# A hybrid attention and expert layer on one core: GpSimd makes each expert tile's low part in two instructions of 512 columns instead of one of 1024

## The chip, the cores and the metric

The kernel runs on one core of a Trainium2 chip. The metric is the device time of one execution in microseconds (us), as the median of several runs. The core has a matrix engine (PE, with its weight loads shown as PEld), a vector engine (DVE), a scalar engine (ACT), GpSimd (POOL) and a queue engine that issues DMAs (SP). They run side by side and wait for one another by semaphores.

## The reference

One layer over 512 tokens of width 1024 in float32: two kinds of attention, an output projection and a layer norm, then an expert layer ("peer") over 16384 experts, each one row of `u` and one of `v`. Cut to the part that matters here:

```python
qb = (xb @ w_q).reshape(TOKEN_BLOCK, PEER_HEADS, 2, PEER_DKEY)
s = jnp.einsum('thcd,hcnd->thcn', qb, sub_keys).astype(jnp.float32)
s_top, i_top = lax.top_k(s, PEER_TOPK)
cand = s_top[:, :, 0, :, None] + s_top[:, :, 1, None, :]
...
best, pos = lax.top_k(cand, PEER_TOPK)
eidx = jnp.take_along_axis(cand_idx, pos, axis=-1)
g = jax.nn.softmax(best, axis=-1)
h = jax.nn.gelu(jnp.einsum('td,thkd->thk', xb, ug).astype(jnp.float32), approximate=False)
return jnp.einsum('thk,thkd->td', (g * h).astype(x.dtype), vg)
```

Per token 16 experts are chosen for each of 8 heads, and their `u` and `v` rows are used. The expert layer's result goes through a last layer norm.

## The kernel before

**Products in three parts.** Each float32 operand of a product is split into a high part (`whi`, `xhi`, made by ACT as a rounded copy) and a low part (`wlo`, `xlo`, the raw value less the high part). The product is the sum of three matmuls: high by high, and twice high by low (`split`, L1306 to L1308).

**The expert stage.** For 384 of the 512 tokens the kernel doesn't gather: it multiplies with all 128 tiles of `u` (128 experts each) and later with all 128 tiles of `v`. A list `SEQ` gives the order of these 256 steps. For each step `s`, SP loads a tile of 128x1024 into `raw` (L513, four slots), ACT makes its high part (`tile_high`, L804), then `tile_low` makes the low part: GpSimd for the first 38 tiles (`POOL_ONLY = 38`, L627), DVE from tile 38 on (L1172). PE waits for the low part (`wait_low`) and runs 24 matmuls of 384 columns (`u_tile`); ACT takes the result through GELU into `hout` (`gelu`, L825) and then makes the high part of the tile four steps ahead. A `u` step of PE lasts 4.16 us.

**Which experts each token wants.** While PE runs the first of these steps, DVE picks the experts: the largest 16 of 128 scores for each head and half (L1078 to L1087), and then `select`, four times (once for each 128 tokens), in six parts. It builds candidate sums (`cand`, L1122), takes the largest 16 (L1126 to L1138), and turns positions into expert numbers by comparisons, products and sums over 128x1920 elements of bf16: `ge` (L1142, L1150), `prod` (L1143, L1147, L1152), `sel` (L1144, L1148, L1153), with short steps between them (L1114, L1140, L1145, L1149, L1154, L1156). DVE's instructions here form one chain in program order.

**What DVE does next.** Behind `select` DVE's program goes on in steps, from step 37: for the first 128 tokens it forms dot products with gathered `u` rows (`dots`, L1180), for which ACT computes the GELU (L840, `dots_gelu`), and adds up `v` rows (`sums`, L1194). It makes the low parts of tiles 38, 39 and so on, and from step 46 one-hot matrices of the chosen experts (`one_hots`, ending in `e1w`, L1211), from which PE forms gate weights (`g_quad`, L1597). ACT's program has `dots_gelu` for step 37 ahead of `gelu(35)`, and PE can't start `u_tile(37)` before `gelu(35)` has emptied its bank of PSUM.

**GpSimd's program in this stage**: `tile_low(0)` to `tile_low(37)`; behind each of `tile_low(26)` to `tile_low(30)` one gather of `u` and `v` rows (L634, an indirect DMA); then 123 further gathers, each waiting for DVE's sums.

Of the kernel before, what the change touches and what calls it, by code (L numbers as in the profile page):

```python
# [23 lines left out]
F32 = mybir.dt.float32  # L24
# [4 lines left out]
ALU = mybir.AluOpType  # L29
# [4 lines left out]
S, D = 512, 1024  # L34
# [127 lines left out]
def program(nc, a):  # L162

    es = ExitStack()
    with es:
# [168 lines left out]
        raw4, whi4, wlo4 = [t[:, :, :].rearrange("p a (b c) -> p (a b) c", b=2) for t in (raw, whi, wlo)]  # L334

        def slot4(n):

            return (n + 2) % 4
# [4 lines left out]
        def sem(name):  # L343
            return es.enter_context(nc.semaphore(name))
# [32 lines left out]
        tile_hi, low_pool, low_dve = sem("tile_hi"), sem("low_pool"), sem("low_dve")  # L377
# [205 lines left out]
        @block.gpsimd  # L583
        def _(pool):
            nc.gpsimd.memset(ident[:, :], 0.0).then_inc(id_steps, 1)
            pool.wait_ge(id_steps, 1)
            nc.gpsimd.affine_select(out=ident[:, :], in_=ident[:, :], compare_op=ALU.not_equal, fill=1.0,
                                    base=0, pattern=[[-1, P]], channel_multiplier=1).then_inc(id_steps, 1)

            def low(g, cols=GC):  # L590

                pool.wait_ge(hi_done, g + 1)
                s = g % 2
                nc.gpsimd.tensor_tensor(wlo[:, s, 0:cols], raw[:, s, 0:cols],  # L594
                                        whi[:, s, 0:cols].bitcast(F32), ALU.subtract).then_inc(lo_done, 1)

            for i in range(4):
                cols = slice(i * GC // 4, (i + 1) * GC // 4)
                if i < 3:
                    pool.wait_ge(first_hi, i + 1)  # L600
                else:
                    pool.wait_ge(hi_done, 1)
                nc.gpsimd.tensor_tensor(wlo[:, 0, cols], raw[:, 0, cols], whi[:, 0, cols].bitcast(F32),
                                        ALU.subtract).then_inc(first_lo if i < 3 else lo_done, 1)
            for g in range(2, G_BR):
                low(g)

            low(G_BR, 6 * 256)
            low(G_BR + 1, 6 * 256)
            for m in range(KD):  # L610
                if m in (2, 4):
                    low(G_BR + m // 2 + 1, 6 * 256)
                pool.wait_ge(mix_hi, m + 1)
                nc.gpsimd.tensor_tensor(xlo[:, m, :], mixa[:, m % 2, :], xhi[:, m, :].bitcast(F32), ALU.subtract).then_inc(mix_lo, 1)
            low(G_WO + 1)
            low(G_WO + 2)
            pool.wait_ge(ln_out, TC)
            for g in range(G_WQ, G_U):
                low(g)

            nc.gpsimd.iota(iota2[:, :, :], [[1, P], [0, 2]], base=0, channel_multiplier=0,
                           allow_small_or_imprecise_dtypes=True).then_inc(iota_done, 1)

            def tile_low(n):

                pool.wait_ge(tile_hi, n + 1)
                nc.gpsimd.tensor_tensor(wlo4[:, slot4(n), :], raw4[:, slot4(n), :], whi4[:, slot4(n), :].bitcast(F32),  # L627
                                        ALU.subtract).then_inc(low_pool, 1)

            def gather(k):  # L630

                if k >= UVB:
                    pool.wait_ge(sum_done, k - UVB + 1)
                nc.gpsimd.indirect_dma_start(  # L634
                    out=uvb[:, k % UVB, :], out_offset=None, in_=a["uv"][:, :],
                    in_offset=bass.IndirectOffsetOnAxis(ap=eidx[:, k:k + 1], axis=0)).then_inc(uv_in[k % UVB], 16)

            for s in range(POOL_ONLY):
                tile_low(s)
                if s == GATHER_TILE:  # L640
                    pool.wait_ge(idx_done, 1)
                if GATHER_TILE <= s < GATHER_TILE + UVB:
                    gather(s - GATHER_TILE)
            for k in range(UVB, NG):
                gather(k)
# [1064 lines left out]
```

## Time and profile before

| what | value |
|---|---|
| median of 3 runs | 1626.87 us (1626.55 to 1627.24) |
| the profiled execution's own time | 1627.04 us |
| its span in the trace | 1624.9 us |
| PE busy | 1607.9 us, 99% of the span |
| DVE busy | 1239.0 us, 76% |
| ACT busy | 637.8 us, 39% |
| POOL busy | 463.7 us, 29% |
| granted PE clock | full speed in every slice of the page |
| L627, the low parts by GpSimd | 38 instructions, 95.0 us, from 494.2 to 652.4 us |

Busy time is the time in which an engine executes instructions. An instruction that stands waiting for a memory port inside the engine is still shown as busy, so that its duration grows; a wait for a semaphore is shown as idle time in front of it.

### The profile page before, as it was taken

To read this page: it belongs to the slowest core of one execution; us is meant where nothing else is said; L and a number is where in the kernel's file an instruction comes from. 1 tells how busy PE (TensorE), PEld (TensorE's weight loads), DVE (VectorE), ACT (ScalarE), POOL (GpSimd) and SP (SyncE) were. 2 spreads that over 40 slices of the span, in tenths; PEclk is the share of its full clock that TensorE was granted. 3 is DMA by queue.
4 is the path that set the end of the run, shared out by engine and by line. 5 is a ranking of instruction groups with operands and counts; after the bars stand their busy time and mean duration, and the time that the engine had idled before them with its cause. 6 is when DMAs were issued, how large, how long until landed. Compare 5 with 4: busy or idle time off the path is not lost.

```text
span 1624.9 us, 24287 instructions
## 1 busy us (share of the span) xinstructions
PE 1607.9 (99%) x9533; PEld 1430.0 (88%) x9533; DVE 1239.0 (76%) x2317; ACT 637.8 (39%) x998; POOL 463.7 (29%) x218
## 2 busy tenths in 40 slices
PE   9999999999999999999999999999999999999997
PEld 8898977888889999999999999999998888888886
DVE  3024366246799999998887799989998898888887
ACT  5324445532223343445455343333333434333332
POOL 4433222351244567300000233333333121222200
PEclk9999999999999999999999999999999999999999
DMA  5332112143124558788788999999999999999961
GB/s 201 146 149 79 55 53 78 59 150 130 53 78 137 177 169 303 275 278 275 245 272 250 402 373 387 396 392 358 357 387 388 366 381 384 373 365 384 392 245 66
DMA packets 135137, 406.56 MB, mean 250 GB/s; under 512 B 10353, under 2 KB 71025, under 8 KB 113777
## 3 DMA queue, kind: packets, MB, share of 16 engines
q1 hardware_dynamic: 116592, 270.80, 46.0%
q0 software_dynamic: 18432, 134.23, 21.0%
q8 instruction: 76, 1.25, 0.3%
q14 instruction: 37, 0.30, 0.1%
HBM read 360.42 MB, written 44.56 MB: 249 GB/s over the span
## 4 chain that ended last, share of the span: by engine, by line
PE 80%; DVE 18%; issue 1%; DMA 1%; POOL 0%; ACT 0%; DVEq 0%; SPq 0%; POOLq 0%
PE bank L1306 24%; PE bank L1308 24%; PE bank L1307 24%; PE bank L1597 3%; DVE idx L1087 1%; DVE idx L1079 1%; DVE val L1078 1%; DVE val L1086 1%; DVE tmp L1080 1%; DVE prod L1143 1%; PE bank L1448 1%; PE bank L1435 1%; DVE prod L1152 1%; PE bank L1405 1%; DVE wlo L1172 1%
## 5 line engine op out<-in xcount | busy, mean ns | idle before, releaser
L1306 PE MATMUL bank<-xhi,whi 128*128 128x384 f32 (+1 forms) x1408 | 499.0, 354 | 1.9 <-ACT hout L825 1.8
L1308 PE MATMUL bank<-xhi,wlo 128*128 128x384 f32 (+1 forms) x1408 | 492.6, 350 | 0.0
L1307 PE MATMUL bank<-xlo,whi 128*128 128x384 f32 (+1 forms) x1408 | 492.0, 349 | 0.0
L634 POOL DMA_INDIRECT uvb<-in_uv,eidx x128 | 201.4, 1573 | 696.8 <-DVE acc L1194 666.3
L804 ACT ACTIVATE whi<-raw 128x1024 fp32r<-128x1024 f32 x256 | 270.2, 1057 | 250.8 <-PE bank L1308 223.5
L1172 DVE TENSOR_TENSOR wlo<-raw,whi 128x1024 fp32r<-128x1024 f32 x218 | 266.0, 1222 | 77.4 <-ACT whi L804 76.8
L1308 PE MATMUL bank<-whi,alo 128*128 128x512 f32 x768 | 299.5, 390 | 0.0
L1307 PE MATMUL bank<-wlo,ahi 128*128 128x512 f32 x768 | 299.4, 390 | 0.0
L1306 PE MATMUL bank<-whi,ahi 128*128 128x512 f32 x768 | 298.7, 389 | 0.0
L1306 PEld LDWEIGHTS bank<-xhi,whi 128*128 128x128 f32 x1408 | 264.5, 188 | 18.5 <-issue 3.5
L1307 PEld LDWEIGHTS bank<-xlo,whi 128*128 128x128 f32 x1408 | 264.6, 188 | 15.2
L1308 PEld LDWEIGHTS bank<-xhi,wlo 128*128 128x128 f32 x1408 | 264.3, 188 | 15.4
L594 POOL TENSOR_TENSOR wlo<-raw,whi 128x2048 fp32r<-128x2048 f32 (+1 forms) x33 | 149.2, 4522 | 298.5 <-ACT whi L654 263.2
L1308 PEld LDWEIGHTS bank<-whi,alo 128*128 128x128 f32 x768 | 144.2, 188 | 29.9
L1306 PEld LDWEIGHTS bank<-whi,ahi 128*128 128x128 f32 x768 | 144.2, 188 | 29.3
L1307 PEld LDWEIGHTS bank<-wlo,ahi 128*128 128x128 f32 x768 | 144.2, 188 | 29.3
L825 ACT ACTIVATE hout<-bank 128x384 f32<-128x384 f32 x128 | 62.8, 491 | 272.2 <-PE bank L1308 270.4
L1194 DVE SCALAR_TENSOR_TENSOR acc<-uvb,hd,acc 128x1024 f32<-128x1024 f32 x127 | 163.2, 1285 | 4.5
L1180 DVE CUSTOM_DVE_ANT_0 uvb<-uvb,xn 128x1024 f32<-128x1024 f32 x128 | 151.3, 1220 | 0.0
L627 POOL TENSOR_TENSOR wlo<-raw,whi 128x1024 fp32r<-128x1024 f32 x38 | 95.0, 2504 | 61.7 <-ACT whi L804 61.6
L847 ACT ACTIVATE ahi<-af 128x384 fp32r<-128x384 f32 x128 | 66.5, 520 | 83.4 <-DVE af L1225 83.4
L1231 DVE TENSOR_TENSOR alo<-af,ahi 128x384 fp32r<-128x384 f32 x128 | 70.7, 552 | 0.0
(197 smaller groups left out, 1742.9 us busy)
## 6 DMA issues: line engine op xcount, KB each, us to landing
raw<-in_u SPq DMA_DIRECT2D x128, 512.0 KB, 6.3
raw<-in_uv SPq DMA_DIRECT2D x128, 512.0 KB, 8.4
g_scratch<-stage SPq DMA_DIRECT2D x48, 512.0 KB, 5.3
gl<-g_scratch SPq DMA_DIRECT2D x32, 768.0 KB, 9.3
raw<-in_w_in SPq DMA_DIRECT2D x22, 1024.0 KB, 4.8
h_scratch<-hout SPq DMA_DIRECT2D x88, 192.0 KB, 4.9
hl<-h_scratch SPq DMA_DIRECT2D x22, 768.0 KB, 10.4
raw<-in_w_q SPq DMA_DIRECT2D x6, 1024.0 KB, 4.8
```

Source lines behind the costliest of these rows:

```text
L594: nc.gpsimd.tensor_tensor(wlo[:, s, 0:cols], raw[:, s, 0:cols], whi[:, s, 0:cols].bitcast(F32), ALU.subtract).then_inc(lo_done, 1)
L627: nc.gpsimd.tensor_tensor(wlo4[:, slot4(n), :], raw4[:, slot4(n), :], whi4[:, slot4(n), :].bitcast(F32), ALU.subtract).then_inc(low_pool, 1)
L634: nc.gpsimd.indirect_dma_start(out=uvb[:, k % UVB, :], out_offset=None, in_=a["uv"][:, :], in_offset=bass.IndirectOffsetOnAxis(ap=eidx[:, ...
L804: nc.scalar.activation(whi4[:, slot4(n), :], raw4[:, slot4(n), :], ACT.Copy).then_inc(tile_hi, 1)
L847: nc.scalar.activation(ahi[:, t % 4, :], af[:, t % 4, :], ACT.Copy).then_inc(a_hi, 1)
L1172: V.tensor_tensor(wlo4[:, slot4(n), :], raw4[:, slot4(n), :], whi4[:, slot4(n), :].bitcast(F32), ALU.subtract).then_inc(low_dve, 1)
L1180: V.tensor_tensor_reduce(out=u, in0=u, in1=xn[:, 0, :], scale=1.0, scalar=0.0, op0=ALU.mult, op1=ALU.add, accum_out=hd[:, k:k + 1]).then_i ...
L1194: V.scalar_tensor_tensor(acc[:, :], v, hd[:, k:k + 1], acc[:, :], ALU.mult, ALU.add).then_inc(sum_done, 1)
L1231: V.tensor_tensor(alo[:, p % 4, :], af[:, p % 4, :], ahi[:, p % 4, :].bitcast(F32), ALU.subtract).then_inc(a_lo, 1)
L1306: mm(out, lh, rh, start=first, stop=False)
L1307: mm(out, lh, rl, start=False, stop=False)
L1308: return mm(out, ll, rh, start=False, stop=last)
```

## The change

In GpSimd's `tile_low`, one subtraction over the tile's 1024 columns becomes two over 512 columns each, in a loop. The first one has no semaphore; the second one carries the increment of `low_pool` that the whole tile had. The wait for ACT's high part stays in front of the first. Nothing else is changed; DVE's own `tile_low` stays whole.

```diff
             def tile_low(n):
 
                 pool.wait_ge(tile_hi, n + 1)
-                nc.gpsimd.tensor_tensor(wlo4[:, slot4(n), :], raw4[:, slot4(n), :], whi4[:, slot4(n), :].bitcast(F32),
-                                        ALU.subtract).then_inc(low_pool, 1)
+                for j in range(2):
+                    o = (slice(None), slot4(n), slice(j * S, (j + 1) * S))
+                    last = nc.gpsimd.tensor_tensor(wlo4[o], raw4[o], whi4[o].bitcast(F32), ALU.subtract)
+                last.then_inc(low_pool, 1)
```

`S` is 512. On GpSimd, the place behind the last weights of the earlier stages and up to the second gather, as the two programs' instructions stand (all line numbers behind L627 are two higher after the change):

```order
 L621 IOTA iota_106 128x256
-L627 TENSOR_TENSOR wlo<-raw,whi 128x1024 x27
-L634 DMA uvb<-in_uv,eidx 128x2048
-L627 TENSOR_TENSOR wlo<-raw,whi 128x1024
...
+L629 TENSOR_TENSOR wlo<-raw,whi 128x512 x54
+L636 DMA uvb<-in_uv,eidx 128x2048
+L629 TENSOR_TENSOR wlo<-raw,whi 128x512 x2
+L636 DMA uvb<-in_uv,eidx 128x2048
```

27 instructions become 54 ahead of the first gather, and two stand between gathers where one stood. The instructions of the other engines and their order stay as they were.

## Rows read from the trace of the kernel before

**Rows 1.** Busy time by stretch: PE, PEld, DVE, ACT, POOL, each with instructions (x)

```profile
494.00:660.00 166.00, 166.00 (x954) 164.23 (x953) 160.15 (x529) 58.75 (x80) 101.57 (x43) 1.00 0.60 194
```

**Rows 2.** PE's waits, whole span: us in total, times, longest

```profile
PE bank L1597 <- DVE e1w L1211: 1.3, 1, 1.3
```

**Rows 3.** Timeline, PE around its first stop: start us, us

```profile
660.63 0.34 PE L1308 MATMUL bank<-xhi,wlo 128*128 128x384 f32 x1
662.80 0.41 PE L1306 MATMUL bank<-xhi,whi 128*128 128x384 f32 x1 [1.83 <-ACT hout L825]
```

**Rows 4.** Timeline, ACT at the same place

```profile
662.08 0.20 ACT L840 ACTIVATE hgel<-hd 128x2 f32<-128x2 f32 x1 [7.95 <-DVE hd L1180]
```

**Rows 5.** The instructions of L627: ns min/median/max; what ended POOL's idle time

```profile
L627 POOL TENSOR_TENSOR wlo<-raw,whi x38: 2382/2392/3531, 494.2 to 650.0; 128x1024 fp32r<-128x1024 f32 x38
...
  ACT whi L804: 61.6, 32
```

**Rows 6.** The instructions of L614, the same operation over 512 columns

```profile
L614 POOL TENSOR_TENSOR xlo<-mixa,xhi x8: 1290/1296/1301, 328.6 to 357.6; 128x512 fp32r<-128x512 f32 x8
```

**Rows 7.** Timeline, DVE, 533 to 659 us

```profile
533.60 3.00 DVE L1122 TENSOR_TENSOR cand<-val 128x64 f32<-128x64 f32 x6
...
544.39 2.16 DVE L1142 TENSOR_TENSOR ge<-bposf,cstb 128x1920 bf16<-128x1920 bf16 x1
546.58 3.31 DVE L1143 TENSOR_TENSOR prod<-ge,didx 128x1920 bf16<-128x1920 bf16 x1
...
566.32 3.19 DVE L1122 TENSOR_TENSOR cand<-val 128x128 f32<-128x128 f32 x7
...
599.40 0.99 DVE L1122 TENSOR_TENSOR cand<-val 128x128 f32<-128x128 f32 x7
...
607.06 0.23 DVE L1140 CAST bposf<-bpos 128x128 bf16<-128x128 uint32 x1
...
654.80 1.23 DVE L1152 TENSOR_TENSOR prod<-ge,didx 128x1920 bf16<-128x1920 bf16 x1
...
658.25 0.29 DVE L1154 TENSOR_TENSOR picks<-sel,idf 128x128 f32<-128x128 f32 x1
```

**Rows 8.** Timeline, POOL, 494 to 627 us

```profile
494.16 4.75 POOL L627 TENSOR_TENSOR wlo<-raw,whi 128x1024 fp32r<-128x1024 f32 x2 [5.78 <-ACT whi L804]
...
546.04 2.77 POOL L627 TENSOR_TENSOR wlo<-raw,whi 128x1024 fp32r<-128x1024 f32 x1 [1.77 <-ACT whi L804]
...
600.12 2.52 POOL L627 TENSOR_TENSOR wlo<-raw,whi 128x1024 fp32r<-128x1024 f32 x1 [1.77 <-ACT whi L804]
...
616.23 0.95 POOL L634 DMA_INDIRECT uvb<-in_uv,eidx  x1 [0.16 <-issue]
...
624.60 1.76 POOL L634 DMA_INDIRECT uvb<-in_uv,eidx  x1
```

**Rows 9.** Groups by form, DVE, 494 to 655 us: busy us, mean ns of one

```profile
L1143 DVE TENSOR_TENSOR prod<-ge,didx 128x1920 bf16<-128x1920 bf16 x4 | 13.2, 3306 | 0.1
L1152 DVE TENSOR_TENSOR prod<-ge,didx 128x1920 bf16<-128x1920 bf16 x4 | 11.1, 2787 | 0.1
...
L1114 DVE TENSOR_TENSOR didx<-idf 128x240 bf16<-128x240 bf16 x4 | 3.3, 817 | 0.1
L1140 DVE CAST bposf<-bpos 128x128 bf16<-128x128 uint32 x4 | 3.2, 805 | 0.1
L1145 DVE TENSOR_TENSOR picks<-sel,idf 128x128 f32<-128x128 f32 x4 | 3.1, 768 | 0.1
...
L1154 DVE TENSOR_TENSOR picks<-sel,idf 128x128 f32<-128x128 f32 x3 | 2.3, 773 | 0.1
L1149 DVE TENSOR_TENSOR jf<-bposf,sel 128x128 bf16<-128x128 bf16 x4 | 2.3, 578 | 0.1
```

**Rows 10.** Timeline, DVE and POOL near 20 us

```profile
18.33 4.36 DVE L898 CAST xplo<-xlo 128x512 fp32r<-128x512 f32 x8
...
21.18 6.00 POOL L594 TENSOR_TENSOR wlo<-raw,whi 128x2048 fp32r<-128x2048 f32 x1 [7.47 <-ACT whi L654]
```

## The prediction

> **What bounds the kernel now.** I read the busy times by stretch first. In the 166 us in which the changed instructions run, PE is busy for all 166.00 us and POOL for 101.57 [rows 1]. So PE doesn't wait for a low part there, and POOL, at 1.77 us idle behind most tiles, has room; what ends its idle time is ACT's high part, 32 times of 38 [rows 5]. A longer or shorter `tile_low` costs PE nothing by itself: a tile is made some three `u` steps (12.5 us) before PE wants it.
>
> But DVE is busy for 160.15 of the 166 us [rows 1], with one chain of instructions, and behind it stand two stops of PE. The first: ACT waited 7.95 us for DVE's dot products, which come straight after `select` [rows 4], so that its GELU came late, and PE started a matmul at 662.80 us whose predecessor had started at 660.63 [rows 3]. Matmuls of this form start 0.17 us apart, so 2.0 us are lost, and 0.1 on the slow first one. The second, 1.3 us, is for DVE's `e1w` [rows 2], some 37 us later in the same unbroken chain. So DVE's arrival at the end of `select` (659.6 us) is on the path. If DVE gets there X earlier, PE gains X, up to 2.1 + 1.3 = 3.4 us; behind that PE alone bounds. If DVE gets there later, PE loses the same, with no cap.
>
> **Why GpSimd's instruction length touches DVE at all.** `prod<-ge,didx` takes 1.23 us when GpSimd is through with its tiles, and 3.31 us at 546.58, as in seven of its eight executions [rows 7, 9]. At 546.04 a low part of GpSimd started; DVE's `ge` (L1142) ran until 546.55; the low part lasts 2.77 us instead of 2.39 and ends at 548.81; DVE's product ends at 549.89, 1.08 us behind it [rows 7, 8]. So each waits for the other's whole instruction: GpSimd 0.4 us for `ge`, then DVE 2.08 us for GpSimd. The two want one thing that only one can hold, and GpSimd had asked for it before the product did. In the Trainium skill, "SBUF — State Buffer", section "Who interferes with whom", this is an exclusive lock on a port pair, taken by a DVE instruction with two SBUF inputs against a GpSimd one that reads SBUF; the rows agree, and the sum by it is the sum below.
>
> What DVE loses so, by its rows in `select` less their own durations: L1143 13.2 - 4 x 1.23 = 8.3; L1152 11.1 - 4 x 1.23 = 6.2; L1114 3.3 - 4 x 0.30 = 2.1; L1140 3.2 - 4 x 0.23 = 2.3; L1145 3.1 - 4 x 0.29 = 1.9; L1154 2.3 - 3 x 0.29 = 1.4; L1149 2.3 - 4 x 0.29 = 1.1 [rows 7, 9]; L1122, whose seven take 0.99 us undisturbed and twice 2.2 us more, 4.4 [rows 7]. Together 27.8 us.
>
> **The change, part by part.**
>
> *GpSimd's own time.* The same operation over 512 columns took 1.29 us [rows 6], over 1024 2.39 [rows 5]: two make 2.58, 0.19 us more per tile, 7 us over 38 tiles. Idle time of 1.77 us per tile hides it; without that cover it would be 7 us. Even if both halves have to let a long DVE instruction through (2.58 + 2.2 + 1.2 = 6.0 us), the tile is done before PE's 12.5 us are over.
>
> *What DVE waits, where it waits.* If DVE, waiting, gets in between the halves, a product's wait falls from 2.08 to what the first half holds: 1.29 less the 0.12 us in which it starts up, less the 0.15 that DVE's own start hides and the 0.03 between DVE's instructions, about 0.98. Seven products: 7 x (2.08 - 0.98) = 7.7 us less.
>
> *What that gives back.* The second half still has to run, and stands waiting when DVE's product ends. It takes the port then, and whatever DVE does 1 to 3 us later meets it. I laid DVE's instructions of 533 to 660 us end to end on this rule, each with its own duration, and GpSimd's halves at ACT's ends, which PE's 4.16 us step fixes. With whole instructions this gives the 23 waits of the trace and its end, 659.6 us. With halves it gives 34 waits: the products fall by 7.7; L1145, L1149 and L1154, short ones behind a product, fall from 4.4 to 2.9; L1140 stays at 2.4. But L1147, which always ran free between two low parts, is met three times (2.9); L1142 and L1150 once each (2.0); L1156 twice (2.2); and the heads of `select` (L1122, L1114), a burst of short instructions that one whole low part stopped three times for 6.5 us, are stopped eight times for 8.7. Sum: -7.7 - 1.5 + 2.9 + 2.0 + 2.2 + 2.2 = +0.1 us, within rounding. DVE ends at 659.8.
>
> *Why the end is so stiff.* After each wait DVE continues when a GpSimd instruction ends, and these stand on PE's 4.16 us grid. So DVE's chain doesn't drift; it comes out at one of a few places. Moving the start-up times and the half's length by a few hundredths left it at +0.1 to +0.2 in most cases, at +0.5 in some, and in some at -3.0 to -3.2, where the last head of `select` slips through. I take +0.1.
>
> *Sum.* 1627.04 (the profiled execution; the median is 0.17 lower) + 0.0 for GpSimd + 0.1 for DVE = 1627.1; against the median, 1627.0 us. Bounds for DVE's term: -3.4 (the cap; all else that it saves finds PE bound) and +3.9 (rival 2).
>
> **The rivals.** *0, the forecast: DVE gets in between the halves, and gives back what it saves.* 1627.0 us. For it: the gather that GpSimd issued right behind a low part at 624.60 took 1.76 us, where the one at 616.23 took 0.95 [rows 8]; a product of DVE that had waited for that low part ran first, and the gather stood behind it. Between two halves GpSimd must start up as well, so a waiting DVE should win.
>
> *1, DVE keeps most of what it saves.* The same mechanism, but the chain comes out a place earlier, 3.1 us or more. PE gains 3.1 to 3.4: 1623.5 to 1623.8. For it: each long wait is halved, and the simplest count (7.7 us less, nothing given back) is far above the cap. Against it: GpSimd's work is as much as before, and DVE's instructions stand too close for the second half to find a gap.
>
> *2, slower: GpSimd doesn't let DVE in between its halves.* The pair then acts as one instruction of 2.53 us, 0.14 longer. For it: the two low parts at 494.16 stand back to back, 4.75 us for both, with no pause [rows 8], and near 20 us it was GpSimd that stood 1.4 us behind three casts of DVE that followed one another without a gap [rows 10]. Most waits would only grow by 0.14 and not add up. The place that decides is 600 us: DVE's seven L1122 at 599.40 just slip through, and the low part of 600.12 waits for them (2.52 instead of 2.39) [rows 7, 8]. DVE 0.02 us or more later is caught there, 2.3 us, and again in the fourth `select`: by the same replay DVE ends at 663.5, +3.9, and PE with it: 1630.8 us. In the Trainium skill, "GPSIMD Engine Reference", section "Instruction dispatch", one of GpSimd's cores may begin the next instruction while others still work on the last, which speaks for this rival (1630.8 us by it); the trace of before has no DVE instruction waiting at such a pair, so it neither agrees nor disagrees.
>
> *3, the split does nothing to the port (it is not held per instruction).* Then DVE's waits follow GpSimd's busy time, 7% more: up to 27.8 x 0.07 = 1.9 us, 1628.8. Against it: waits end 1.08 us behind a low part's end each time.
>
> **How the numbers follow.** Forecast 0: 0.55. Rival 1: 0.22. Rival 2: 0.15. Rival 3 and small shifts the other way (+0.5 to +2 us): 0.08. A measurement of this kernel tells about 0.2%, 3.25 us, from no change. Rival 1 lies right at that bound (3.1 to 3.4), so I give it half to "faster": with a little for a place further up, 0.13. Slower is rival 2 and a little more: 0.17. Within: 0.70. The range holds forecast 0, rival 1 and the small shifts, and leaves rival 2 out: 1623.4 to 1628.2; the forecast alone would be 1626.5 to 1627.6.
>
> **What would show it.** Right: 76 instructions of 512 columns near 1.28 us; L1143 and L1152 at about 2.2 us instead of 3.31; some L1147, L1142 or L1156 a microsecond longer than before; the first dot product (L1182 then) near 659.8; PE's stops still near 1.8 and 1.3. Products that stay at 3.3 or go to 3.45 would show rival 2; dot products near 656.5 or earlier and PE's two stops gone, rival 1. The forecast is wrong if the replay's rule of who goes first is wrong, for a single burst that slips through moves the end by a whole place.

## The result, and the profile after

The changed kernel takes 1631.10 us (median of 10 runs, 1630.75 to 1632.34); beside it the kernel before took 1627.05 us (1626.55 to 1627.4). The ratio is 1.0027 with a 95% interval of 1.0019 to 1.0034: 4.05 us or 0.27% slower. The profiled execution took 1630.99 us, its span is 1628.8 us, 3.9 more than before.

Read first, as before, the busy times by stretch (PE, PEld, DVE, ACT and POOL with their instructions, then the granted clock):

```profile
494.00:660.00 166.00, 166.00 (x954) 164.19 (x953) 160.32 (x523) 58.91 (x80) 112.97 (x81) 1.00 0.60 194
660.00:665.00 5.00, 1.17 (x7) 0.84 (x5) 4.83 (x9) 0.00 (x0) 0.00 (x0) 0.81 0.01 2
665.00:668.00 3.00, 1.36 (x4) 1.39 (x5) 2.66 (x5) 2.08 (x5) 0.62 (x1) 0.50 0.00 0
668.00:672.00 4.00, 4.00 (x19) 4.00 (x19) 4.00 (x6) 0.77 (x1) 3.20 (x2) 0.76 0.48 133
```

Up to 660 us nothing happens to PE: 166.00 us busy with the same 954 matmuls as in [rows 1], although POOL is busy for 11.4 us more. All is lost behind 660 us, and the clock falls there, to 0.50 for 3 us. PE's waits from 490 to 720 us have one row where there were two (1.8 us, and 1.3 for `e1w` [rows 2]):

```profile
PE bank L1308 <- ACT hout L827: 5.5, 1, 5.5
```

PE's timeline around that stop, to be read against [rows 3]:

```profile
660.83 0.34 PE L1310 MATMUL bank<-xhi,wlo 128*128 128x384 f32 x1
666.64 0.66 PE L1308 MATMUL bank<-xhi,whi 128*128 128x384 f32 x1 [5.48 <-ACT hout L827]
667.10 0.52 PE L1309 MATMUL bank<-xlo,whi 128*128 128x384 f32 x1
667.42 0.52 PE L1310 MATMUL bank<-xhi,wlo 128*128 128x384 f32 x1
```

The gap between the starts is 5.81 us; it was 2.17. Behind it matmuls start 0.32 us apart, where before the change they started 0.17 to 0.18 apart at the same place. ACT says what PE stood for (compare [rows 4]):

```profile
665.92 0.20 ACT L842 ACTIVATE hgel<-hd 128x2 f32<-128x2 f32 x1 [11.60 <-DVE hd L1182]
```

So the question goes to DVE. Two rows of its timeline before the change, which stand for what follows:

```profile
615.04 1.20 DVE L1145 TENSOR_TENSOR picks<-sel,idf 128x128 f32<-128x128 f32 x1
...
659.67 1.23 DVE L1180 CUSTOM_DVE_ANT_0 uvb<-uvb,xn 128x1024 f32<-128x1024 f32 x1
```

Its timeline after the change, first at a product, then at the two rows that matter, and last at the first dot product, which starts 3.83 us later:

```profile
609.71 2.19 DVE L1145 TENSOR_TENSOR prod<-ge,didx 128x1920 bf16<-128x1920 bf16 x1
611.93 2.15 DVE L1146 TENSOR_REDUCE sel<-prod 128x128 f32<-128x1920 bf16 x1
614.12 2.75 DVE L1147 TENSOR_TENSOR picks<-sel,idf 128x128 f32<-128x128 f32 x1
...
627.33 5.23 DVE L1156 TENSOR_TENSOR picks<-sel,idf 128x128 f32<-128x128 f32 x1
...
663.50 1.22 DVE L1182 CUSTOM_DVE_ANT_0 uvb<-uvb,xn 128x1024 f32<-128x1024 f32 x1
```

The product takes 2.19 us instead of 3.31 [rows 7], which is the 0.98 us of waiting that was forecast. But an instruction of 0.29 us takes 2.75 and another 5.23. GpSimd's timeline at the same moments:

```profile
608.65 4.40 POOL L629 TENSOR_TENSOR wlo<-raw,whi 128x512 fp32r<-128x512 f32 x2 [0.36 <-ACT whi L806]
613.20 0.95 POOL L636 DMA_INDIRECT uvb<-in_uv,eidx  x1 [0.15 <-issue]
614.17 2.54 POOL L629 TENSOR_TENSOR wlo<-raw,whi 128x512 fp32r<-128x512 f32 x2
...
626.42 0.95 POOL L636 DMA_INDIRECT uvb<-in_uv,eidx  x1 [0.16 <-issue]
627.39 5.01 POOL L629 TENSOR_TENSOR wlo<-raw,whi 128x512 fp32r<-128x512 f32 x4
```

Both long rows of DVE start within 0.1 us of the end of a gather (L636), with halves straight behind it, and both end 0.16 us behind the last half of the row: two halves at 614.17 (end 616.71; DVE 616.87), four at 627.39 (two tiles, since GpSimd was late; end 632.40; DVE 632.56). DVE did not get in between them. They cost 2.46 and 4.94 us. I subtracted from each DVE instruction the duration of its form when GpSimd is out of the way: before, 23 waits sum to 27.9 us; now 31 sum to 31.6, and in the other 29 DVE got in at the end of the half that it met. In 15 of these it met the first half of a tile, with the second directly behind, and got in between; only these 15 tell something about the step between halves.

### The profile page after: what moved, and what is told of

It is laid out like the page before. It is cut to its first block, busy times and chain, and to the rows that moved or that the text cites. A ratio compares the mean times of both kernels' runs of the same rounds, so it can differ in the third digit from the quotient of the medians.

```text
span 1628.8 us, 24325 instructions
## 1 busy us (share of the span) xinstructions
PE 1609.2 (99%) x9533; PEld 1431.4 (88%) x9533; DVE 1242.4 (76%) x2317; ACT 637.9 (39%) x998; POOL 475.8 (29%) x256
## 4 chain that ended last, share of the span: by engine, by line
PE 82%; DVE 16%; issue 1%; DMA 1%; POOL 0%; ACT 0%; DVEq 0%; SPq 0%; POOLq 0%
PE bank L1308 25%; PE bank L1310 25%; PE bank L1309 25%; PE bank L1599 3%; DVE idx L1089 1%; DVE idx L1081 1%; DVE val L1080 1%; DVE val L1088 1%; DVE tmp L1082 1%; PE bank L1450 1%; PE bank L1437 1%; PE bank L1407 1%; DVE cand L1124 1%; DVE ge L1144 1%; DVE prod L1145 1%
## 5 line engine op out<-in xcount | busy, mean ns | idle before, releaser
L636 POOL DMA_INDIRECT uvb<-in_uv,eidx x128 | 200.8, 1569 | 699.3 <-DVE acc L1196 665.4
L629 POOL TENSOR_TENSOR wlo<-raw,whi 128x512 fp32r<-128x512 f32 x76 | 108.1, 1444 | 50.5 <-ACT whi L806 50.1
```

The lines of the kernel that those rows point to most:

```text
L629: last = nc.gpsimd.tensor_tensor(wlo4[o], raw4[o], whi4[o].bitcast(F32), ALU.subtract)
L636: nc.gpsimd.indirect_dma_start(out=uvb[:, k % UVB, :], out_offset=None, in_=a["uv"][:, :], in_offset=bass.IndirectOffsetOnAxis(ap=eidx[:, ...
```

## The experiments

Each was timed beside the kernel before, whose median was 1627.0 to 1627.2 us each time. "First dot product" is the start of DVE's L1180 or what became of it: 659.67 us before, 663.50 after.

**1. Semaphore waits between GpSimd's halves.** Each half waits for the one ahead of it to have completed.

```diff
+                if n >= 1:
+                    pool.wait_ge(low_pool, n)
                 for j in range(2):
                     ...
+                    if j == 0:
+                        last.then_inc(low_half, 1)
+                        pool.wait_ge(low_half, n + 1)
```

> Halves as in the change, but GpSimd waits for its own last subtraction before each next one, so that two halves never stand back to back. Theory A (the 3.8 us that DVE lost come from two waits, 2.3 and 4.9 us, in which DVE was shut out over two and four halves that followed one another without a pause behind a gather): no wait of DVE is longer than one half, 1.3 us; the first dot product comes at 660 us or earlier instead of 663.5; time 1623.7 to 1627.3 us. Theory B (halves cost DVE in general, by more frequent meetings, wherever they stand): the dot product stays near 663.5 or later, 1630 to 1632 us. Theory C (the loss is GpSimd's own longer time): the waits make it longer still, over 1631 us.

Measured: 1627.97 us (1.0012, interval 1.0003 to 1.0021). The runs fall into two groups: seven of eleven took 1627.5 to 1628.2 us, four took 1630.5 to 1632.0, as long as the changed kernel. The trace is of one of the seven (1627.69 us): first dot product at 660.36, PE's first stop 2.5 us. What the four did is not known. The place of the first long row, DVE and then GpSimd:

```profile
614.06 1.50 DVE L1153 TENSOR_TENSOR picks<-sel,idf 128x128 f32<-128x128 f32 x1
```

```profile
613.13 0.95 POOL L642 DMA_INDIRECT uvb<-in_uv,eidx  x1
614.10 2.68 POOL L632 TENSOR_TENSOR wlo<-raw,whi 128x512 fp32r<-128x512 f32 x2
```

The same meeting, 0.04 us apart and behind a gather, now costs 1.21 us instead of 2.46: DVE goes in at the first half's end (615.40). Its longest wait anywhere is 1.66 us: it began at 628.04, during a gather that ended at 628.50, and DVE got in only behind the half that followed the gather. In this trace no wait spans two halves, so the shutting-out over a whole row needs halves that stand back to back. The time came out a little above what I expected, since 33 waits still sum to 28.6 us.

**2 and 3. Halves for tiles 0 to 25 only, and for tiles 26 to 37 only.** The gathers stand behind tiles 26 to 30.

```diff
-                for j in range(2):
-                    o = (slice(None), slot4(n), slice(j * S, (j + 1) * S))
+                parts = 2 if n < GATHER_TILE else 1      # experiment 3: n >= GATHER_TILE
+                for j in range(parts):
+                    o = (slice(None), slot4(n), slice(j * D // parts, (j + 1) * D // parts))
```

> Halves for tiles 0 to 25 only, whole low parts from tile 26 on, where the gathers begin. Theory A: no wait of DVE over more than one instruction of GpSimd (longest 2.3 us, behind a whole one); first dot product at 660.5 or earlier; 1623.7 to 1627.5 us. Theory B: most of the loss stays, since two thirds of the halves do: 1629 to 1631.5 us.

> The other part alone: whole low parts for tiles 0 to 25, halves from tile 26 on, behind which the gathers stand. Theory A: at least one wait of DVE of 2.2 us or more that ends behind the second or a later half of a row without pause; first dot product 1 to 4 us later than in the kernel before; 1628 to 1631.5 us. Theory B: a third of the loss at most, 1627 to 1628.5 us, and no wait over 1.3 us.

Measured: the early halves 1626.76 us (0.9998, 0.9989 to 1.0007), first dot product at 659.36; the late ones 1631.17 us (1.0025, 1.0015 to 1.0035), at 662.92, with a PE stop of 5.5 us. DVE in experiment 3:

```profile
613.54 2.76 DVE L1148 TENSOR_TENSOR picks<-sel,idf 128x128 f32<-128x128 f32 x1
...
626.77 5.23 DVE L1157 TENSOR_TENSOR picks<-sel,idf 128x128 f32<-128x128 f32 x1
```

The twelve late tiles make the whole loss, with the same two rows. The 26 early ones, two thirds of the change, do what was forecast: less waiting in each product, all of it given back, nothing at the end.

**4. GpSimd almost out of the way.** One subtraction over 32 columns of each tile; the other 992 columns of the low part are left out.

```diff
-                nc.gpsimd.tensor_tensor(wlo4[:, slot4(n), :], raw4[:, slot4(n), :], ...)
+                o = (slice(None), slot4(n), slice(0, 32))
+                nc.gpsimd.tensor_tensor(wlo4[o], raw4[o], whi4[o].bitcast(F32), ALU.subtract).then_inc(low_pool, 1)
```

> GpSimd's low part covers only the first 32 of each tile's 1024 columns, so most of the low part of tiles 0 to 37 is left out and DVE is almost never in its way. If DVE's arrival at the end of select is what PE feels, DVE comes some 25 us earlier, both of PE's stops in the expert stage are gone, and the time falls by 3.4 us, no more: 1623.5 to 1623.9 us. If PE's stops have another cause, the time stays within 1 us of 1627.

Measured: 1623.31 us (0.9976, 0.9967 to 0.9986). DVE's waits fall to 0.2 us in all, and the first dot product moves 28 us forward:

```profile
631.35 1.23 DVE L1180 CUSTOM_DVE_ANT_0 uvb<-uvb,xn 128x1024 f32<-128x1024 f32 x1
```

Both of PE's stops are gone. So 28.3 us of DVE are worth 3.8 us of time: that is the cap on anything that helps DVE here.

**5. Does DVE have to be first?** One rival for the shutting-out: DVE came 0.05 us *ahead* of the half and lost a tie. The other: the gather ahead of the halves is what matters. A short dummy instruction in DVE's chain puts L1147 (L1154 here) behind the half's start. The kernel also has two small index fills on GpSimd, behind its last gather and so far from this place.

```diff
+                    if c == 2:
+                        step(V.max(cand2[:, 0, 0:8], cand[:, 0, :]))
```

> The changed kernel, and in the third of DVE's four selects one idle maximum over 50 columns ahead of the short product that was shut out over two halves. That product started 0.05 us ahead of GpSimd's first half; now it starts some 0.2 us behind that start, with the same gather ahead and the same two halves back to back. Theory A1 (what shuts DVE out is the start in the same moment as a row of GpSimd instructions): it gets in behind the first half, its wait falls from 2.5 to 1.1 us, and the places behind it shift by 1 us, so that the wait of 4.9 us most likely goes too: 1626.5 to 1628.5 us. Theory A2 (what shuts DVE out is the gather ahead of the halves, wherever DVE starts): it still waits for both halves, 2.2 us, and the time stays at 1630.5 to 1632 us. Two index fills by GpSimd behind the last gather only give their durations.

Measured: 1630.85 us (1.0024, 1.0014 to 1.0034), first dot product at 662.91. DVE, then GpSimd:

```profile
613.63 2.51 DVE L1154 TENSOR_TENSOR picks<-sel,idf 128x128 f32<-128x128 f32 x1
```

```profile
612.46 0.95 POOL L637 DMA_INDIRECT uvb<-in_uv,eidx  x1
613.43 2.55 POOL L630 TENSOR_TENSOR wlo<-raw,whi 128x512 fp32r<-128x512 f32 x2
```

DVE now starts 0.20 us *behind* the first half and is still kept out of both; the later long row (5.24 us at 626.59) is there too. The tie is refuted; the gather stands.

**6. The same five gathers seven tiles later**, with halves, and in **10** with whole low parts.

```diff
-GATHER_TILE = 26
+GATHER_TILE = 33
```

> The changed kernel with the first five gathers behind tiles 33 to 37 instead of 26 to 30. Both forms of theory A: without gathers GpSimd keeps to its 4.16 us grid from 605 to 633 us, and both long waits there are gone (longest wait before 635 us at most 1.3 us). In the new place of the gathers, 640 to 660 us, there are fewer of DVE's instructions left to meet; one new long wait at most. Time 1626.5 to 1629 us. Theory B (halves cost by more frequent meetings): 1630 to 1632 us.

> Whole low parts, gathers behind tiles 33 to 37: the control for the halves with the same place of the gathers (1624.9 us). If halves gain where no gather stands between them, whole low parts give more: DVE's first dot product at 659 us or later instead of 657.1, 1626 to 1628 us. If that gain was the place of the gathers alone, 1624.5 to 1625.3 us.

Measured: halves 1624.93 us (0.9990, 0.9981 to 0.9999; nine runs at 1624.2 to 1625.3, two at 1627.3 and 1627.8, of which there is no trace), first dot product at 657.06; whole 1625.36 us (0.9991, 0.9982 to 1.0000), at 658.10. DVE in experiment 6, at the old place and at the new one of the gathers:

```profile
613.32 0.33 DVE L1147 TENSOR_TENSOR picks<-sel,idf 128x128 f32<-128x128 f32 x1
...
642.44 2.76 DVE L1147 TENSOR_TENSOR picks<-sel,idf 128x128 f32<-128x128 f32 x1
```

```profile
641.52 0.95 POOL L636 DMA_INDIRECT uvb<-in_uv,eidx  x1
642.49 2.55 POOL L629 TENSOR_TENSOR wlo<-raw,whi 128x512 fp32r<-128x512 f32 x2
```

The long rows left with the gathers, and one came up where the gathers went. The time was below what I had expected, and experiment 10 says why: moving the gathers gives 1.65 us by itself, so experiment 6 measures two things. Between whole and halves with the gathers there, 0.43 us are inside what a measurement can tell.

**7 and 8. A sum step fewer ahead of `gelu(35)`.** If only DVE's late arrival at its dot products costs PE, then moving the first of them behind PE's need should free the kernel of it. The first entry of the list of sum steps goes; all sums are still made, one more in the next stretch. In 7 the low parts are whole, in 8 in halves.

```diff
-SUM_STEPS = [37, 39, 42, 44] + [83 + i * 87 // 38 for i in range(38)] + [172 + i * 78 // 22 for i in range(22)]
+SUM_STEPS = [39, 42, 44] + [83 + i * 87 // 39 for i in range(39)] + [172 + i * 78 // 22 for i in range(22)]
...
-            for s in range(SUM_STEPS[0], 2 * NT):
+            for s in range(POOL_ONLY - 1, 2 * NT):
```

> The kernel before, with whole low parts, but only three of the 64 pairs of dot products and sums ahead of step 46 (steps 39, 42, 44 instead of 37, 39, 42, 44; the next 39 spread over the steps where 38 stood). DVE has 5 us less to do ahead of its one-hot matrices, and ACT asks for the first dot products two steps later, so both of PE's stops should be gone: 1623.2 to 1624 us, as with the low part left out. If there is another stop behind these two, or the denser sums later cost something, 1624.5 to 1627.5 us.

> The same three sums with the halves of the change. DVE may still lose up to 4 us to its waits, but PE no longer waits for the end of select within that margin: the loss of the change disappears, 1623.2 to 1624.5 us, within 0.7 us of the kernel with whole low parts. If the halves cost something by another way than DVE's late end of select, 1627 us or more.

Measured: 7 takes 1623.42 us (0.9977, 0.9968 to 0.9986), 8 takes 1625.34 us (0.9989, 0.9980 to 0.9998). Of PE's waits in 8:

```profile
PE bank L1599 <- DVE e1w L1213: 1.5, 1, 1.5
```

In 7 both stops are gone, and PE is busy for all of 494 to 672 us. In 8 the stop for ACT is gone, but the one for `e1w` is there with 1.5 us: the two long rows still stand in DVE's chain (2.75 us at 613.52, 5.23 at 626.72), and their delay reaches `e1w`, 37 us further on. I had expected halves not to matter any more with this order; they cost 1.9 us. DVE's lateness is carried on as long as its chain has no gap.

**9 and 11. A wait behind each gather only.** The halves stay back to back. Behind each of the five gathers GpSimd clears one column of a buffer that is dead by then, and waits for that to have completed. In 11 the order of experiment 7 is added.

```diff
                     gather(s - GATHER_TILE)
+                    nc.gpsimd.memset(squares[:, 0:1], 0.0).then_inc(met, 1)
+                    pool.wait_ge(met, s - GATHER_TILE + 1)
```

> The changed kernel, and behind each of the five gathers between tiles one fill of a single column by GpSimd, for whose end GpSimd waits before it goes on to the next tile. The halves stay back to back, within a tile and from tile to tile. Theory A2a (behind a gather GpSimd's cores are out of step, run through the halves behind one another, and never leave the port free until the row ends; a common wait puts them in step): no wait of DVE is longer than one half, 1.3 us, and the time is 1625 to 1628 us, as with waits between all halves (1628.0) or better. Theory A2b (any row of halves with no pause that follows a gather shuts DVE out, in step or not): the waits of 2.5 and 4.9 us stay, 1630.5 to 1632 us.

> Halves, three sums ahead of step 46, and the fill and wait behind each gather. With them in step, DVE is not shut out, and PE's stop of 1.5 us at the one-hot matrices goes: 1623.0 to 1624.0 us, the same as whole low parts with three sums (1623.4). If the fill doesn't help, 1625.3 us as without it.

Measured: 9 takes 1626.94 us (1.0000, 0.9991 to 1.0009), first dot product at 659.20; 11 takes 1623.43 us (0.9978, 0.9969 to 0.9987). GpSimd and DVE in 9:

```profile
612.41 0.95 POOL L637 DMA_INDIRECT uvb<-in_uv,eidx  x1 [0.15 <-issue]
613.37 0.11 POOL L647 MEMSET squares<- 128x1 f32 x1
613.56 3.52 POOL L630 TENSOR_TENSOR wlo<-raw,whi 128x512 fp32r<-128x512 f32 x2
```

```profile
613.32 0.29 DVE L1150 TENSOR_TENSOR picks<-sel,idf 128x128 f32<-128x128 f32 x1
613.65 2.27 DVE L1152 TENSOR_TENSOR prod<-ge,cstb 128x1920 bf16<-128x1920 bf16 x1
...
618.47 3.21 DVE L1155 TENSOR_TENSOR ge<-jf,cstb 128x1920 bf16<-128x1920 bf16 x1
```

The short instruction that was shut out before now starts at 613.32, just ahead of the gather's end, and runs freely, since the half comes 0.19 us later. The product behind it starts at 613.65, 0.09 us behind the first half, about as DVE did in experiment 5 (0.20 us), and gets in at that half's end: 2.27 us, 1.04 of waiting. At 618.47 it is again 0.09 us behind a half (618.38) and waits 1.05 us. Its longest wait in the stage is 1.14 us. Five such pauses, 0.19 us from the gather's end to the first half, take all 4.1 us of the loss away, with every half still in place. Whether by the wait itself or by the later start of the halves, this run doesn't separate: in all three close meetings (613.65, 618.47 and 628.99) another DVE instruction with two inputs was running when the first half began; in the shut-out ones there was none.

## Why the prediction was wrong

**What held.** *GpSimd's own time*: 1292 ns a half, and PE busy for all of 494 to 660 us. POOL's busy time rose by 11.4 us, not 7; halves that stood waiting for DVE took up to 2375 ns. The row of L629 shows both (ns min/median/max):

```profile
L629 POOL TENSOR_TENSOR wlo<-raw,whi x76: 1281/1292/2375, 494.4 to 651.5; 128x512 fp32r<-128x512 f32 x76
```

*What DVE waits*: seven products were to lose 7.7 us. DVE's groups by form from 494 to 663 us (busy us, mean ns), against [rows 9]:

```profile
L1144 DVE TENSOR_TENSOR ge<-bposf,cstb 128x1920 bf16<-128x1920 bf16 x4 | 9.6, 2404 | 0.1
L1145 DVE TENSOR_TENSOR prod<-ge,didx 128x1920 bf16<-128x1920 bf16 x4 | 8.8, 2197 | 0.1
...
L1152 DVE TENSOR_TENSOR ge<-jf,cstb 128x1920 bf16<-128x1920 bf16 x4 | 8.6, 2158 | 0.1
...
L1149 DVE TENSOR_TENSOR prod<-ge,cstb 128x1920 bf16<-128x1920 bf16 x4 | 7.8, 1958 | 0.1
L1154 DVE TENSOR_TENSOR prod<-ge,didx 128x1920 bf16<-128x1920 bf16 x4 | 7.8, 1952 | 0.1
...
L1156 DVE TENSOR_TENSOR picks<-sel,idf 128x128 f32<-128x128 f32 x4 | 6.4, 1593 | 0.1
...
L1147 DVE TENSOR_TENSOR picks<-sel,idf 128x128 f32<-128x128 f32 x4 | 4.5, 1128 | 0.1
L1158 DVE TENSOR_TENSOR picks<-best 128x128 f32<-128x128 f32 x4 | 3.3, 830 | 0.0
...
L1151 DVE TENSOR_TENSOR jf<-bposf,sel 128x128 bf16<-128x128 bf16 x4 | 2.5, 630 | 0.1
```

And the groups before the change that [rows 9] do not hold, from 494 to 660 us:

```profile
L1142 DVE TENSOR_TENSOR ge<-bposf,cstb 128x1920 bf16<-128x1920 bf16 x4 | 8.6, 2158 | 0.1
L1150 DVE TENSOR_TENSOR ge<-jf,cstb 128x1920 bf16<-128x1920 bf16 x4 | 8.6, 2158 | 0.1
...
L1147 DVE TENSOR_TENSOR prod<-ge,cstb 128x1920 bf16<-128x1920 bf16 x4 | 4.9, 1228 | 0.1
...
L1154 DVE TENSOR_TENSOR picks<-sel,idf 128x128 f32<-128x128 f32 x4 | 2.6, 652 | 0.1
...
L1156 DVE TENSOR_TENSOR picks<-best 128x128 f32<-128x128 f32 x4 | 1.1, 281 | 0.0
```

L1145 fell from 13.2 to 8.8 and L1154 from 11.1 to 7.8: 7.7 us. *What that gives back*: L1149 rose from 4.9 to 7.8 (forecast 2.9 us) and L1158 from 1.1 to 3.3 (forecast 2.2), both to the tenth; L1144 and L1152 together rose by 1.0 where 2.0 were forecast. The heads of `select` (L1124 and L1116 now) went from 6.5 us of waiting to 6.7, where 8.7 were forecast. (The prediction's eight terms of what DVE lost before add to 27.7 us, not 27.8; nothing hangs on it.)

**The step that failed** stands under *what DVE waits*: "If DVE, waiting, gets in between the halves". I took that for every meeting. It is true in 29 of 31, of which 15 put it to the test. In the other two a gather ran directly ahead of the row of halves, and DVE was kept out of the whole row. They fall on L1147 and L1156, which with L1151 were to go from a wait of 4.4 to 2.9 us; the busy time of the three was 8.0 us before (3.1 + 2.3 + 2.6) and is 13.4 now (4.5 + 2.5 + 6.4), 5.4 more where 1.5 less were forecast. That is 6.9 us; the sum for DVE was off by only 3.6 (3.7 against 0.1), because the heads of `select`, L1144 with L1152, and L1142 came out 3.3 us below their forecast together. The evidence that I gave for the step, the gather behind a low part at 624.60 [rows 8], is a case of DVE against a gather that *follows*; none had a gather in front of a row of low parts, and I didn't look for what differs there.

The meeting is no accident either, and could have been worked out. A product that DVE gets in between the halves ends at 611.90. From there DVE's reduction, which does not meet GpSimd, takes 2.15 us, and L1147 starts at 614.12. From the same moment GpSimd has its second half (ends 613.05), 0.15 us, and the gather of 0.95 us: 614.15. The paths are 2.2 us both. So the split itself puts DVE's next two-input instruction on the gather's end; again from 625.11 us. Before, DVE's product went behind the *whole* low part, and the gather stood behind the product for 1.76 us [rows 8]; no such meeting was there.

**The mechanism.** Shown: it came and went with the gathers (experiment 6), it needs no tie (5), and with semaphore waits of GpSimd between all halves (1, as traced) or once behind each gather (9) no DVE instruction was shut out over a row. A gather directly ahead isn't enough, though. In the changed kernel another gather runs from 620.68 to 621.63, with halves straight behind it:

```profile
621.65 4.61 POOL L629 TENSOR_TENSOR wlo<-raw,whi 128x512 fp32r<-128x512 f32 x2
```

```profile
620.73 2.16 DVE L1152 TENSOR_TENSOR ge<-jf,cstb 128x1920 bf16<-128x1920 bf16 x1
622.92 2.19 DVE L1154 TENSOR_TENSOR prod<-ge,didx 128x1920 bf16<-128x1920 bf16 x1
```

Here the product got in between the halves, with 0.97 us of waiting. DVE's `ge` was running when the row began, and the first half had to let it end. The same happens in experiments 3, 5, 6 and 8 (622.34, 622.16, 651.22, 622.31). In the nine shut-out meetings DVE ran a reduction or a maximum, which take the same time whether GpSimd works or not, when the first half began or just before.

In the Trainium skill, "GPSIMD Engine Reference", section "Instruction dispatch", consecutive GpSimd instructions are no barrier between its cores, and only who waits for an instruction's semaphore is held until all are done. That fits: if the gather leaves the cores out of step, some are always inside the next half when others end, so that the port is never free to DVE until the row ends, and a wait, or a half that stands behind DVE, brings them together. No row here shows single cores, so this last part is argued, not shown.

**Rival 2** had the number, 1630.8 us, and DVE's arrival at the end of `select`, 663.5 against a forecast of 659.8; it was given 0.15. But it came there another way. It had GpSimd keep DVE out of *every* pair, and the loss come from a slip of 0.02 us near 600 us. Products of 2.20 us refute the first, and experiment 3, with no halves at 600 us and the same loss, the second.

**From DVE to PE.** "If DVE gets there later, PE loses the same, with no cap" came out near (DVE 3.83 us later, span 3.9), by terms that I had not counted. PE's first stop grew by 3.64 us (5.81 less 2.17). The clock at half speed then cost about 1.5: in the 166 us before, matmuls stand 0.17 us apart, then some ten of them 0.32. Against that the second stop of 1.3 us is gone, since PE was now late for `e1w` too. 3.64 + 1.5 - 1.3 = 3.8. *The cap*, which I put at 3.4 us, is 3.8 (experiments 4 and 7 with 1623.31 and 1623.42 us): a term mis-sized by 0.4, which also made me put rival 1 right at the bound of what can be told.

**The forecast with the failed step mended** is experiment 9: 1626.94 us, where 1627.0 was forecast for DVE getting in at each half. DVE's waits sum to 28.2 us there, where 28.0 were forecast; but the heads of `select` take 6.7 of them and not 8.7, so that the near agreement is in part luck.

## What to carry to other kernels

Splitting an instruction to shorten another engine's wait can give nothing if the work behind the wait still has to pass the same port: here the saved time came back (DVE's waits sum to 28.0 us in experiment 2, 27.9 before), and two unlucky meetings made it a loss. Where GpSimd issues a gather ahead of port-using instructions while DVE's chain is on the path, try a semaphore wait behind the gather, as in experiment 9. Better, find what is late behind the chain: leaving GpSimd whole and moving one sum step past PE's need (experiment 7) removed both stops and gave 1623.42 us, 0.23% below the kernel before and 0.47% below the changed one.

## What the chip showed that I had not expected

- A waiting DVE instruction got the port at the end of the first of two GpSimd instructions standing back to back (a product waited 0.97 us for halves of 1.29). It did not where the halves stood directly behind a gather and began while DVE held nothing that they wanted: then it waited for two halves (2.2 to 2.5 us) or four (4.94 us), in all nine such meetings of the changed kernel and experiments 3, 5, 6 and 8.
- A stop of PE of 5.5 us was followed by a granted clock of 0.50 (1.2 of 2.4 GHz), with matmuls 0.32 us apart instead of 0.17; behind stops of 1.8 to 2.5 us there was none of it: in experiment 9, with a stop of 2.0 us, the clock is 1.00 in each stretch from 660 to 672 us. The last row of the first fence shows it recovering, with 19 matmuls in 4 us; the same stretch of the kernel before has 25.
